# Order of output product, modulation steps, squares and gathers in a hybrid layer kernel with expert lookup

## The reference

```python
sh1, sc1, g1, sh2, sc2, g2 = modulation(cvec, w_mod, b_mod)      # 1024 -> 6 x 1024
h = modulate(x, norm1, sh1, sc1)
u, c_q, c_kv, k_rope = split(h @ w_in)
ssm_out = yg * sigmoid(yg @ w_glu)          # yg = gelu(S5 scans of u)
attn = attend(q, k, v)                      # latent attention, 8 heads
x = x + g1 * (concat(ssm_out, attn) @ w_out)
h2 = modulate(x, norm2, sh2, sc2)           # rmsnorm(x) * norm2 * (1 + sc2) + sh2
# peer: 8 heads x 16 picks per token out of 16384 experts
s = (h2 @ w_query) . sub_keys               # 2 x 128 scores per head
top_s, top_i = top_k(s, 16)                 # per half
best, pos = top_k(top_s[0] + top_s[1], 16)  # over 256 pairs
idx = top_i[0] * 128 + top_i[1]; g = softmax(best)
x = x + g2 * sum_k gelu(h2 . u_table[idx_k]) * g_k * v_table[idx_k]
y = rmsnorm(x, final_norm)
```

## Time and profile before

| | us |
|---|---|
| median of 3 runs | 841.61 |
| lowest, highest | 840.71, 841.67 |
| the profiled execution | 841.02 |
| its span, first to last instruction | 839.2 |
| TensorE matmul busy | 707.3 |
| VectorE busy | 591.4 |
| ScalarE busy | 334.6 |
| GpSimd busy | 377.2 |
| gathers: share of 16 DMA engines' span | 77.6% |
| plain loads: share of 16 DMA engines' span | 16.3% |

### The profile page before, as it was taken

The page is one execution under the profiler, slowest core; times in us unless marked ns, Lnnn a source line. Parts: engine busy times, 40 slices in busy tenths (PEclk is TensorE's granted clock), DMA queues, the critical chain, the costliest instruction groups (busy, mean ns, idle before and its releaser), DMA issues. The chain is left out here.

```text
span 839.2 us, 10338 instructions
## 1 busy us (share of the span) xinstructions
PE 707.3 (84%) x3385; PEld 352.9 (42%) x3385; DVE 591.4 (70%) x1284; ACT 334.6 (40%) x995; POOL 377.2 (45%) x335
## 2 busy tenths in 40 slices
PE   3899999999978988899869787777877877877784
PEld 0586666656434455677524232323322222322221
DVE  7979623677995658958898856887687578744544
ACT  3423351345466324433344433353334333433331
POOL 3628900244535453444465544446444444455500
PEclk9999999999999999999999999998999999999999
DMA  9956697989999999999999999999999999999992
GB/s 349 419 205 230 224 378 267 351 316 406 419 422 371 422 424 368 422 421 422 387 418 423 422 422 422 422 423 421 422 422 424 421 422 422 422 422 422 422 423 93
DMA packets 50270, 321.74 MB, mean 383 GB/s; under 512 B 9948, under 2 KB 10652, under 8 KB 12200
## 3 DMA queue, kind: packets, MB, share of 16 engines
q0 software_dynamic: 36864, 268.45, 77.6%
q1 hardware_dynamic: 12984, 52.44, 16.3%
q10 hardware_dynamic: 368, 0.18, 0.1%
HBM read 318.77 MB, written 1.23 MB: 381 GB/s over the span
## 5 line engine op out<-in xcount | busy, mean ns | idle before, releaser
L845 PE MATMUL psum<-mem 128*128 128x512 f32 x868 | 429.1, 626 | 95.4 <-ACT mem L1232 95.0
L1507 POOL DMA_INDIRECT mem<-uv_table,small x232 | 279.1, 1203 | 292.4 <-PE psum L845 226.9
L1857 DVE CUSTOM_DVE_ANT_0 mem<-mem,h 128x1024 f32<-128x1024 f32 x232 | 282.6, 1225 | 148.4 <-DMA mem<-uv_table,small 143.3
L845 PEld LDWEIGHTS psum<-mem 128*128 128x128 f32 x868 | 156.6, 195 | 337.0 <-ACT mem L1232 205.4
L1221 ACT ACTIVATE small<-small 128x1 f32<-128x1 f32 x252 | 50.9, 202 | 282.2 <-DVE small L1857 279.4
L1232 ACT ACTIVATE mem<-consts,small 128x128 f32<-128x128 f32 x238 | 95.6, 402 | 7.9
L1226 ACT ACTIVATE small<-small 128x1 f32<-128x1 f32 x256 | 75.4, 294 | 26.3 <-DVEq L1850 3.0
L792 PEld LDWEIGHTS psum<-hT,mem 128*128 128x128 f32 x352 | 42.3, 193 | 11.3 <-issue 7.7
L1507 POOL DMA_INDIRECT spare_page<-uv_table,small x24 | 28.3, 1178 | 40.9 <-PE psum L845 26.7
L1422 POOL TENSOR_SCALAR small<-small 128x1 f32<-128x1 f32 (+1 forms) x9 | 4.6, 514 | 92.0 <-DVE small L1887 44.7
L792 PE MATMUL psum<-hT,mem 128*128 128x128 f32 x352 | 42.4, 276 | 3.4 <-DMA mem<-w_query 3.4
(11 more groups left out here) (239 smaller groups left out, 731.9 us busy)
## 6 DMA issues: line engine op xcount, KB each, us to landing
mem<-w_mod SPq DMA_DIRECT2D x24, 1024.0 KB, 9.6
mem<-w_query SPq DMA_DIRECT2D x6, 1024.0 KB, 9.2
mem<-w_out SPq DMA_DIRECT2D x4, 1024.0 KB, 7.2
mem<-uv_table,small POOLq DMA_INDIRECT x232, 25.8
mem<-w_in_u SPq DMA_DIRECT2D x2, 1024.0 KB, 14.7
late<-w_query SPq DMA_DIRECT2D x2, 1024.0 KB, 9.6
mem<-w_in_qkv SPq DMA_DIRECT2D x2, 1008.0 KB, 12.5
mem<-w_ukv SPq DMA_DIRECT2D x1, 1024.0 KB, 8.3
```

Of the source, the lines that this page charges most:

```text
L845: mm = pe.matmul(bank(f"acc_{g}_{half}"), diag[:, pick % DEEP, :], row_of(pick)[:, D + 512 * half:D + 512 * half + 512], start=first, stop ...
L1507: pool.indirect_dma_start(row_of(pick), None, uv_table, bass.IndirectOffsetOnAxis(ap=idx[:, pick:pick + 1] if pick else first_idx, axis=0) ...
L1857: dve.tensor_tensor_reduce(out=row[:, 0:D], in0=row[:, 0:D], in1=h[:, pick // PICKS, :], scale=1.0, scalar=0.0, op0=ALU.mult, op1=ALU.add, ...
```

## The change

On TensorE the second half of prompt's output product (`out_projection(0, half, range(4))`) is issued ahead of `pair_step("a", 2)` and `("a", 3)`. The sample's gate is issued in three pieces. The first scores come right behind the first queries; the mod2b steps, latents and the second half of queries are spread behind them, and `out_projection(1)` waits for `ssm_ready` 2 on TensorE, where ScalarE had that wait. Prompt's squares are formed by halves: columns 0 to 511 by ScalarE once the first residual is added, the others by VectorE, and GpSimd puts them together. VectorE does `norm_columns` after that, computes the index of the second pick by itself (`second_number`: the pair 0,1 or 1,0, whichever sum is larger), and does `gated(1)` after the gates of the first head. Queries of the first head lie in other memory (`first_qT`), some PSUM banks change, mod2b.1 and mod2b.3 load into page LATE2 and query1.0 after them, and the list of free pages has another order.

```diff
-PAGES += [(f"mod2b.{i}", (15, 3)[i % 2]) for i in range(4)]
+PAGES += [(f"mod2b.{i}", (15, LATE2)[i % 2]) for i in range(4)]
...
-    free = [SPARE, 15, 3, 4, 5, 2, 13]
+    free = [SPARE, 3, 4, 15, 5, 2, 13]
...
-    order += [("mix_0_0", 0), ("mix_0_1", 7), ("mq2a", 3), ("mcs", 1), ("mcc", 2), ("glu1", 6), ("cq_1", 4), ("kv_1", 5),
-              ("h2T_0_0", 1), ("h2T_0_1", 2), ("mq2b", 3), ("qry_0_0a", 6), ("sc_0_0a", 7), ("qry_0_0b", 1), ("sc_0_0b", 2),
-              ("hlast", 7), ("back_0_0", 6), ("back_0_1", 7), ("mix_1_0", 2), ("mix_1_1", 6)]
+    order += [("mix_0_0", 0), ("mix_0_1", 7), ("mq2a", 3), ("mcs", 1), ("mcc", 2), ("glu1", 0), ("cq_1", 4), ("kv_1", 5),
+              ("h2T_0_0", 1), ("h2T_0_1", 2), ("mq2b", 3), ("qry_0_0a", 6), ("sc_0_0a", 6), ("qry_0_0b", 1), ("sc_0_0b", 2),
+              ("hlast", 6), ("back_0_0", 7), ("back_0_1", 7), ("mix_1_0", 2), ("mix_1_1", 6)]
...
             load("mod2b.0")
             load("mod2b.1")
-            load("query1.0")
-            load("mod2b.2")
             sp.wait_ge(sq2_ready, 1)
             load("query1.1")
+            load("mod2b.2")
             load("mod2b.3")
+            load("query1.0")
...
             out_projection(0, 0, range(4, 8), first=True)
             out_projection(0, 1, range(4, 8), first=True)
+            pe.wait_ge(ssm_ready, 1)
+            out_projection(0, 0, range(4), last=True)
+            out_projection(0, 1, range(4), last=True)
             pair_step("a", 2)
             pair_step("a", 3)
-            pe.wait_ge(ssm_ready, 1)
-            out_projection(0, 0, range(4), last=True)
+            gate_projection(1, (0,))
             columns_turned()
-            out_projection(0, 1, range(4), last=True)
-            gate_projection(1, (0, 1, 2, 3))
-            pair_step("b", 0)
             normed_turned(0, 0)
             normed_turned(0, 1)
+            gate_projection(1, (1,))
+            first_queries()
+            turned_back(0, 0)
+            first_scores(0)
+            gate_projection(1, (2, 3))
+            pair_step("b", 0)
             pe.wait_ge(y_read, NC)
-            latents(1, (0,))
-            first_queries()
+            latents(1, (0, 1, 2))
+            second_queries()
+            first_scores(1)
             pair_step("b", 1)
-            first_scores(0)
-            second_queries()
             pair_step("b", 2)
-            first_scores(1)
+            latents(1, (3, 4, 5))
             finish(pe.transpose(start("hlast")[0:2 * DT, 0:P], hlast, ident), "hlast")
-            turned_back(0, 0)
             turned_back(0, 1)
             pair_step("b", 3)
-            latents(1, (1, 2, 3, 4, 5, 6, 7))
+            latents(1, (6, 7))
+            pe.wait_ge(ssm_ready, 2)
             for half in range(2):
                 out_projection(1, half, range(4), first=True)
...
             gate_evac(0)
             act.dma_start(new_ckv, ckv_out).then_inc(ckv_stored, 16)
             act.dma_start(new_krope, krope[:, 0, :]).then_inc(ckv_stored, 16)
+            act.wait_ge(low_added, 1)
+            act.activation(low_squares, x[:, 0, 0:512], ACT.Square, accum_out=ms_low).then_inc(low_squared, 1)
             evacuate(modrow[:, 2, :], bank("mq2a"), "mq2a")
-            gate_evac(1)
             root_spread(0)
             normed_evac(0, 1)
-            act.wait_ge(ssm_ready, 2)
             first_query(0)
             first_scored(0)
+            gate_evac(1)
             first_query(1)
             first_scored(1)
             wait_filled(act, "hlast")
...
                 elif page_ == 3:
-                    pool.wait_ge(mod_used, MOD.index("mod2b.3") + 1)
+                    wait_filled(pool, "glu1")
...
-                elif pick == 1 or pick % BATCH == 0:
+                elif pick == 1:
+                    pool.wait_ge(second_ready, 1)
+                elif pick == 2 or pick % BATCH == 0:
                     pool.wait_ge(idx_ready, pick // BATCH + 1)
...
-            inverse_root(rstd_2[:, 0:1], ms_2[:, 0:1], [(0, 1, D)], sq2_ready, 1, rstd2_ready)
+            pool.wait_ge(low_squared, 1)
+            step(pool.tensor_scalar(ms_low, ms_low, 1.0 / D, EPS, ALU.mult, ALU.add))
+            pool.wait_ge(sq2_ready, 1)
+            step(pool.tensor_scalar(ms_2[:, 0:1], ms_2[:, 0:1], 1.0 / D, ms_low, ALU.mult, ALU.add))
+            pool.tensor_tensor(rstd_2[:, 0:1], ms_2[:, 0:1], half_neg[:, 0:1], ALU.pow).then_inc(rstd2_ready, 1)
...
+            def second_number():
+                other = slice(1, None, -1)
+                tt(second_sums, tops[:, 0, 0:2], tops[:, 1, other], ALU.add)
+                step(dve.scalar_tensor_tensor(second_numbers, topi[:, 0, 0:2], float(NKEYS), topi[:, 1, other], ALU.mult, ALU.add))
+                tt(second_lead, second_sums[:, 0:1], second_sums[:, 1:2], ALU.is_ge)
+                tt(second_gap, second_numbers[:, 0:1], second_numbers[:, 1:2], ALU.subtract)
+                dve.scalar_tensor_tensor(second_idx, second_gap, second_lead, second_numbers[:, 1:2], ALU.mult, ALU.add).then_inc(second_ready, 1)
...
             gated(0)
+            residual(0, 0)
+            dve.sem_inc(low_added, 1)
+            residual(0, 1)
+            prompt_squares()
             norm_columns()
-            residual(0, 0)
-            residual(0, 1)
-            square_sum(0)
-            gated(1)
             normed_first()
             tables_first(0, (0, 1))
             dve.scalar_tensor_tensor(first_idx, topi[:, 0, 0:1], float(NKEYS), topi[:, 1, 0:1], ALU.mult, ALU.add).then_inc(first_ready, 1)
+            second_number()
             tables_second((0, 1))
             pairs_first((0, 1))
             number(0, (0, 1), (0, 8))
             pairs_second(0, (0, 1))
             number(0, (0, 1), (8, TOPK))
             normalise(0, 0, (0, 1))
+            gated(1)
```

More of the change, by code:

```diff
@@ L207, in layer @@
         first_idx = part(1).bitcast(U32)
+        second_idx = part(1).bitcast(U32)
+        second_sums, second_numbers, second_gap, second_lead = part(2), part(2), part(1), part(1)
         inner, half_dot = part(1), part(1)
@@ L826, in score_parts @@
                 for i in parts:
-                    mm = pe.matmul(out[:, P * i:P * i + P], qryT[:, i, :], keys_sb[:, 4 * n + i, :], start=True, stop=True)
+                    mm = pe.matmul(out[:, P * i:P * i + P], turned[:, i, :], keys_sb[:, 4 * n + i, :], start=True, stop=True)
                 finish(mm, name)
@@ L835, in first_scores @@
                 wait_emptied(pe, f"qry_0_0{'ab'[half]}")
-                score_parts(f"sc_0_0{'ab'[half]}", 0, range(2 * half, 2 * half + 2))
+                score_parts(f"sc_0_0{'ab'[half]}", 0, range(2 * half, 2 * half + 2), first_qT)
             def accumulate(pick):
@@ L1195, in first_query @@
                 name, two = f"qry_0_0{'ab'[half]}", slice(2 * half, 2 * half + 2)
-                evacuate(qryT[:, two, :], bank(name).rearrange("p (i n) -> p i n", i=4)[:, two, :], name)
+                evacuate(first_qT[:, two, :], bank(name).rearrange("p (i n) -> p i n", i=4)[:, two, :], name)
             def first_scored(half):
```

16 lines of the change are left out of this document (13 added, 3 removed).

## The result

The changed kernel takes 847.52 us (median of 7 runs, 846.40 to 853.18), the kernel before in the same series 841.61 (7 runs, 840.71 to 843.11): ratio 1.0082, 95% interval 1.0063 to 1.0102. It is slower by 5.9 us, where 3.0 were forecast. The profiled execution took 846.93, its span is 845.1 against 839.2.

A forecast was written before the change was run, and what follows sets the result against it. Transfers bound the kernel from about 200 us, TensorE's full list its start. First accumulation 4.85 us later, less 1.5 slack and 0.35 from the thin stretch, gives +3.0 us: 841.61 becomes 844.6, range 843.0 to 846.6.

The forecast's parts named there:

- the wider one: The range 839.8 to 847.0 us, reaching from inside the rival that it evens out.
- the sentence that lets norm_columns hold nothing but `normed_first`: Ahead of the first queries: norm_columns, behind squares and columns, takes 2.0 us, so normed_first begins at 140.1 us.
- the 1.5 us of slack: Gather at 211.98 lands after 7.3 us against 5.8 for an empty queue, so a later TensorE reaches the stream less 1.5.
- SyncE's queue: Loads of query0.1, keys and mod2b.0 go later but stay hidden, by 2.6 to 3.2 us.
- what is late next: Before out_projection(1): TensorE, through with the last latents at 170.8 us, waits for sample's gate and starts at 172.3.
- rival of a larger wait: mod2b.3 lands 2 to 3 us later, or ScalarE needs 1.4 more before the exponential: 846.0 to 847.6; chance 0.12.
- a drain on ScalarE: Second case of the larger-wait rival: 1.38 us after the table load delays the exponential and the end, to 846.0.
- absorption: Behind the first accumulation: 0 to 1.6 us of the lateness come back before the end; 0.35 taken.
- the thin stretch: 240 to 262 us, DMA at 391 GB/s instead of 421: the only place that gives time back, at most 1.6 us.
- +4.85: First accumulation at 179.2 us instead of 174.33, since out_projection(1) starts at 172.3 instead of 167.46.
- The lead: Rival: early gathers fill DMA time at 150 to 165 us, the saturated part begins 3.7 us sooner: 837.9; chance 0.14.
- even out: Rival: waits ahead of out_projection(1) overlap more, slack takes 1.5 us and the thin stretch the rest: 841.6; chance 0.14.

The follow-up runs named there:

- banks: Changed kernel with h2's transposes in PSUM banks 4 and 5 and the wait for y_read ahead of them; 847.80 us against 842.05 for the kernel before.
- exp_first: Changed kernel with ScalarE's exponential of the first gates ahead of the last bias copy; 847.90 us against 842.05 for the kernel before, ratio 1.0063.
- aw_page: all_waits with the old order of free pages (15 first); 842.82 us against 842.06 for the kernel before, ratio 1.0014.
- delay kernels: Kernel before with 4 or 10 added matmuls ahead of out_projection(1); 845.42 and 850.43 us against 842.05.
- delay10: Kernel before with ten added matmuls of 512 columns ahead of out_projection(1); 850.43 us against 842.05, ratio 1.0102.
- all_waits: exp_first with the edits of banks and back_bank and the last mod2b step behind out_projection(1); 841.66 us, as the kernel before, and 842.56 against 842.06 in a second series.
- the two series: all_waits against itself without second-pick index and new page order: shifts 0.0 and +3.2 us on two chips, +0.5 and +1.6 on one.
- free_old: Changed kernel with the old order of free pages (15 ahead of 3 and 4); 847.53 us against 841.29 for the kernel before, ratio 1.0068.
- late kernels: The four mod2b steps moved to picks 88, 93, 98 and 102: 849.41 us on the kernel before (ratio 1.0093), 847.79 on all_waits (1.0076).
- back_bank: Changed kernel with turned_back(0,1) in bank 1 instead of 7; 847.73 us against 841.23 for the kernel before, ratio 1.0066.

## Why the prediction was right or wrong

Direction and path held. The median, 847.5, is 0.9 us above the forecast's own range (843.0 to 846.6) and 0.5 above the wider one that it also gives (to 847.0). Two steps failed: the sentence that lets norm_columns hold nothing but `normed_first`, and the 1.5 us of slack; and mod2b.3's time to land was mis-sized. In us behind the output product:

| step | forecast | measured |
|---|---|---|
| `normed_turned` | 18.0 | 20.2 |
| first gather | 29.3 | 30.6 |
| second gather behind it | 1.5 | 1.5 |
| mod2b.3 issued | 39.0 | 40.1 |
| mod2b.3, issue to landing | 7.3 | 8.2 |
| last step ends | 48.2 | 50.3 |
| from there to the first product | 3.6 | 3.6 |
| `out_projection(1)` | 52.0 | 54.0 |
| first accumulation | 58.9 | 61.0 |

**Up to the first gather.** Squares by halves, the residual, GpSimd's pieces and the columns came as worked out; the banks kernel, without the bank wait, has the norm at 18.0 and the gather at 29.4. The step that failed here is the sentence on norm_columns. I let it set `normed_first` on VectorE, and didn't ask whose banks the transposes write. `mcs` and `mcc` lie in 1 and 2, as `h2T_0_0` and `h2T_0_1` do; before, norm_columns ran at 134.30 to 136.28, long before the norm, and the shared banks cost nothing. The change moves the reader behind the squares and makes the bank a wait of 2.01 us. SyncE's queue: hidden, as forecast.

**Behind it.** The chain from the last step to the first product is right to 0.1 us, and so is "what is late next": without the gate's wait `out_projection(1)` gains 1.3 us (exp_first), where 1.5 were worked out. The last step is 2.1 us later than forecast: 1.1 from mod2b.1's later use, which is what is left of the bank wait, and 0.9 from the landing. The row that I took it from the earlier trace rows had one gather beside it; now 8.2, 8.6 in banks, and 4.7 in aw_page, where no gather is ahead of it. That is the mechanism of the rival of a larger wait, whose prices 846.0 to 847.6 hold the result and to which I gave 0.12; but it asked for a landing 2 to 3 us later, and 0.9 came, so that its number fits is in part luck. Its other branch, a drain on ScalarE, didn't happen: the exponential starts 0.01 us behind the load (172.79 + 1.28 = 174.07, then 174.08). The Trainium skill (ScalarE: Activation LUTs, "What ACT_TABLE_LOAD costs") counts 1.38 us more there; the trace doesn't agree, before or after the change.

**Slack and absorption.** 1.85 us were to be lost on the way. The delay kernels give back 0.2 of 8.6 us and nothing of 3.4, so the slack step is wrong: the gather that should have landed 3.3 us later lands 8.8 later. A landing time says how long a transfer queued and not how much later its issue could be. In the changed kernel 7.0 at the entry became 5.9 and 6.8 at the end. In its profile the landings lag by 8.9 us at gather 60, 7.0 at gather 65 and 5.8 at gather 95, so what came back did so there; in the second profile of the same kernel they are 7.1, 7.3 and 6.1, so only the later part repeats, the one that goes with the new list of pages. In the thin stretch nothing did: it moved along, as thin as before (392 against 391 GB/s), because its cause is late by as much. The kernel before stands there for an index itself (gather at 331.25, wait of 5.81 us on VectorE). delay10, as late, gets nearly nothing back at these places; it has the old list. The part at gathers 60 to 65, in one profile of two, stays open.

**The sum.** +4.85 should have been +7.0: 2.1 of the 2.9 us that the median lies off. The other 0.8 are the 1.85 us of slack and absorption, of which 1.1 or less came about.

**The other rivals.** The lead didn't survive: it needed TensorE at its list without a wait, and even all_waits, which has that, only comes level. It didn't even out: the waits came to more than was summed, not to less. That the early gathers bring no time was right for the changed kernel, by two terms that I didn't see, 1.4 us lost at the entry and about 1.2 won at gathers 90 to 105; with the waits gone they and the page order bring 1 to 3 us, if the two series are taken at their medians.

## What to carry to other kernels

Where one engine works off a full list ahead of a saturated loop, a later entry shifted the end nearly one for one (8.6 us gave 8.4, 3.4 gave 3.4), and the list's length with its waits is what to count; a transfer's queueing time is no slack. When work is moved, list for each moved result which bank it writes, who has to read that bank first, and where that reader now stands; a wait that an old order hid comes out. Waits shade each other: one removed alone brought nothing measurable (2.0 and 1.8 us here), all of them together brought 6 us, so read such an edit by the entry into the loop and by the end together, since free_old enters 1.4 us sooner than the changed kernel and gains nothing, and the late kernels enter 3 and 4 us sooner than the one before and lose. Don't move loads out of idle transfer time to shorten the list, and ask of an early gather which load it delays.

## What the runs showed of the hardware

In the changed kernel TensorE's granted clock held at 1.00 through waits of 1.77 and 1.35 us, some two us apart. In banks it went to 0.50, the level of 1.2 GHz, over 168 to 172 us behind 1.77 and 1.75 us; in back_bank, with one wait of 2.60, it was 0.90 and then 0.76 in the two stretches of 5 us, and six matmuls took 2.47 us instead of 1.43. In back_bank it fell behind the bank wait too (0.67 over 140 to 145 us), and behind the same wait in the changed kernel it held. So the length of a wait alone doesn't say whether the clock falls. Where it fell, the six matmuls of the last step took 1.0 to 1.3 us longer, which is part of why banks and back_bank enter so late in their profiles.

A plain load of 1 MB that takes 4.8 us (mod2b.3 in aw_page, 4.7) took 7.5 to 8.6 beside gathers: 7.5 in back_bank, 8.2 in the changed kernel, 8.6 in banks. The kernels that load 4 MB in the full stream instead of in a stretch with room lose 7.6 and 7.8 us over these loads.
